# Delta rule inverse on 64 by 64 diagonal blocks in opposite quarters of TensorE, with a later channel mean and six earlier taps

## The reference

```
def gated_delta_rule_chunked(q, k, v, g, beta):
    ...
    L = jnp.where(strict, jnp.einsum('nbhid,nbhjd->nbhij', kb, kc) * decay, 0.0)
    eye = jnp.eye(CHUNK, dtype=jnp.float32)
    rhs = jnp.concatenate([vc * bc[..., None], kb * jnp.exp(gc)[..., None]], axis=-1)
    sol = lax.linalg.triangular_solve(eye + L, rhs, left_side=True, lower=True, unit_diagonal=True)
    ...

def hybrid_mixer(...):
    ...
    c = jax.nn.glu(cfm_in, axis=-1)
    c = causal_dwconv(c, cfm_dw_w) + cfm_dw_b
    c = jax.nn.silu(layernorm(c, cfm_ln_g, cfm_ln_b))
    return jnp.concatenate([o_gdn, c], axis=-1) @ w_out
```

## Time and profile before

| | us |
|---|---|
| median of 3 runs | 2077.14 |
| lowest and highest run | 2076.63, 2080.01 |
| the profiled execution, its own time | 2076.46 |
| its span (first to last instruction) | 2074.7 |
| TensorE busy in the span | 2043.9 |
| the inverse, from the last gdn tile to `within(0)` | 1381.1 to 1439.7 |
| the state loop, to the first channel matmul | 1439.7 to 1477.35 |

### The profile page before, as it was taken

How to read it: one execution, slowest core, us unless ns; L and a number is a source line. 1 busy time by engine, 2 the same in 40 slices (tenths; PEclk the granted TensorE clock), 3 DMA queues, 4 the chain that set the end, 5 groups by cost and what they waited for, 6 DMA issues and landing times.

```text
span 2074.7 us, 27847 instructions
## 1 busy us (share of the span) xinstructions
PE 2043.9 (99%) x10022; PEld 1670.7 (81%) x10022; DVE 926.3 (45%) x1180; ACT 891.8 (43%) x1094; POOL 897.8 (43%) x412
## 2 busy tenths in 40 slices
PE   9999999999999999999999999999999999999998
PEld 5888878787878788888888887788898778888887
DVE  4344434354545444511113247877571267555313
ACT  4566652323232332433332247687653335444321
POOL 3232234342424244444444447769265134444443
PEclk9999999999999999999999999999999999999999
DMA  8121123433343332232332332210244123232331
GB/s 332 60 63 60 61 77 111 142 106 142 106 140 107 137 96 91 85 98 91 101 100 93 111 93 70 71 62 2 80 144 124 39 82 100 93 96 96 101 102 61
DMA packets 56383, 203.78 MB, mean 98 GB/s; under 512 B 6256, under 2 KB 8432, under 8 KB 54896
## 3 DMA queue, kind: packets, MB, share of 16 engines
q1 hardware_dynamic: 56304, 202.70, 29.6%
HBM read 200.57 MB, written 2.10 MB: 98 GB/s over the span
## 4 chain that ended last, share of the span: by engine, by line
PE 78%; issue 8%; DVE 5%; POOL 5%; ACT 3%; DMA 0%; POOLq 0%; DVEq 0%; SPq 0%; ACTq 0%
PE acc L2045 18%; PE acc L2047 18%; PE acc L2046 18%; PE aux L2045 5%; PE aux L2047 4%; PE aux L2046 4%; POOL w_lo L525 3%; POOL cfy L550 2%; PE acc L2346 2%; PE aux L2244 1%; DVE qkvf L1718 1%; PE aux L2242 1%; PE aux L2336 1%; PE aux L2257 1%; PE acc L2231 1%
## 5 line engine op out<-in xcount | busy, mean ns | idle before, releaser
L525 POOL TENSOR_TENSOR w_lo<-raw,w_hi 128x1024 fp32r<-128x1024 f32 x317 | 773.6, 2445 | 1123.8 <-ACT w_hi L584 1123.0
L584 ACT ACTIVATE w_hi<-raw 128x1024 fp32r<-128x1024 f32 x317 | 335.3, 1060 | 538.8 <-PE acc L2047 402.2
L2045 PE MATMUL acc<-x_hi,w_hi 128*128 128x512 f32 (+1 forms) x1336 | 523.9, 392 | 6.0 <-DVE x_lo L1463 2.2
L2047 PE MATMUL acc<-x_hi,w_lo 128*128 128x512 f32 (+1 forms) x1336 | 517.7, 387 | 0.0
L2046 PE MATMUL acc<-x_lo,w_hi 128*128 128x512 f32 (+1 forms) x1336 | 517.1, 387 | 0.0
L2045 PEld LDWEIGHTS acc<-x_hi,w_hi 128*128 128x128 f32 x1336 | 251.3, 188 | 62.4 <-DVE x_lo L1463 4.8
L2047 PEld LDWEIGHTS acc<-x_hi,w_lo 128*128 128x128 f32 x1336 | 251.1, 188 | 52.0
L2046 PEld LDWEIGHTS acc<-x_lo,w_hi 128*128 128x128 f32 x1336 | 251.4, 188 | 49.9 <-issue 0.5
L1491 DVE TENSOR_TENSOR ht<-acc,tn 128x512 f32<-128x512 f32 x21 | 14.5, 691 | 173.9 <-PE acc L2047 171.3
L1220 DVE SCALAR_TENSOR_TENSOR adac<-ada,c_act,adac 128x1024 f32<-128x1024 f32 x28 | 40.5, 1446 | 91.9 <-DMA ada<-in_ada 91.4
L2045 PE MATMUL aux<-x_hi,w_hi 128*128 128x512 f32 x192 | 74.9, 390 | 0.8 <-POOL w_lo L525 0.8
(11 more groups left out here) (520 smaller groups left out, 3621.0 us busy)
## 6 DMA issues: line engine op xcount, KB each, us to landing
raw<-in_weights SPq DMA_DIRECT2D x324, 512.0 KB, 3.6
ada<-in_ada SPq DMA_DIRECT2D x32, 512.0 KB, 3.7
ada<-in_ada_first SPq DMA_DIRECT2D x8, 1024.0 KB, 12.1
resid<-in_x SPq DMA_DIRECT2D x2, 1024.0 KB, 6.3
out<-resid SPq DMA_DIRECT2D x16, 128.0 KB, 1.7
decay<-in_tables SPq DMA_DIRECT2D x4, 256.0 KB, 3.4
memf<-in_mem SPq DMA_DIRECT2D x1, 1024.0 KB, 5.1
angles<-in_tables SPq DMA_DIRECT2D x1, 512.0 KB, 4.0
```

Source lines behind the costliest of these rows:

```text
L525: nc.gpsimd.tensor_tensor(lo_home(u), raw[s][:], hi_home(u).bitcast(F32), ALU.subtract).then_inc(lo_ready, 1)
L584: return nc.scalar.activation(out, in_, func, **kw)
L2045: M(out, a_hi, b_hi, start=first, stop=False)
L2047: return M(out, a_lo, b_hi, start=False, stop=last)
```

## The change

The inverse is taken on two 64 x 64 diagonal blocks per chunk and head. The five lower levels work on each block alone: every product becomes two matmuls with 64 rows, 64 weight columns and 64 data columns, one in the upper left quarter of the array, one in the lower right. `xm`, `zs` and the new `xp` hold the blocks packed, 256 columns instead of 512. The transposes become matmuls with the identity. Up to level 4 `x_new` goes into the packed `xp`; the last copies go back to `xt` in two halves. In the last level only the block below the diagonal is computed, in one quarter, scaled by -1 and copied into `xt`.

The taps are spread anew: ScalarE and POOL take three instead of two in each of the conv tiles k = 6 to 11, ScalarE one instead of 1 or 2 in each step of the inverse, and the rest in the state loop. VectorE does fewer in the inverse and more before `within(1)`. `channel_mean` moves from c = 1 to c = 2, `channel_squares` from c = 2 to c = 3, with the steps of ScalarE and VectorE that belong to them.

```
-TN_TAPS, LATE_TAPS = 8, 42
+MORE_FROM = 6
+TN_TAPS, LATE_TAPS = 8, 48
...
+HB = P // 2
+PACK = GDN_H * HB
...
# halves
+    for l in range(1, LEVELS - 1):
+        halves[HB:P, l * P:l * P + HB] = halves[HB:P, l * P + HB:(l + 1) * P]
...
# POOL
-                    cfm_taps(EARLY_POOL)
+                    cfm_taps(EARLY_POOL + (KVQ + MORE_FROM <= j - AHEAD < GATE))
...
# ScalarE, conv tiles
-                cfm_taps(EARLY_POOL)
+                cfm_taps(EARLY_POOL + (k >= MORE_FROM))
...
-                        own["x_first"].own(f(xm[:, c, :], aux[:, c * T:(c + 1) * T]))
+                        own["x_first"].own(f(xm[:, c, :], aux[:, c * T:c * T + PACK]))
...
+            def take_turned(n):
+
+                c, turned = n % NB, aux[:, (4 + n % 2) * T:(4 + n % 2) * T + PACK]
+                own["x_turned"].next()
+                if n < (LEVELS - 3) * NB:
+                    own["x_new"].own(f(xp[:, c, :], turned))
+                    return
+                for r in QUARTER:
+                    ins = f(xt[c].rearrange("p (h n) -> p h n", h=GDN_H)[r, :, r],
+                            turned[r, :].rearrange("p (h n) -> p h n", h=GDN_H))
+                    (own["x_new"] if r.start else step).own(ins)
...
-                cfm_taps(2 if n % 4 else 1)
+                cfm_taps(1)
                 if n < (LEVELS - 2) * NB:
-                    own["x_turned"].next()
-                    own["x_new"].own(f(xt[n % NB], aux[:, (4 + n % 2) * T:(5 + n % 2) * T]))
-
-
-            cfm_taps(len(taps))
+                    take_turned(n)
+
...
# ScalarE, state loop
             new_values(0)
             w_turned(1)
+            cfm_taps(2)
             take_output(0)
+            cfm_taps(2)
             new_values(1)
             w_turned(2)
+            cfm_taps(2)
             output_root(0)
             take_output(1)
+            cfm_taps(len(taps))
             output_hi(0)
             new_values(2)
             w_turned(3)
+            output_root(1)
+            take_output(2)
+            output_hi(1)
+            new_values(3)
             for k in range(CFM_T):
                 own["cfc_ready"].next()
                 own["cfsq_ready"].own(f(cfin[:, k, 0:T], cfy[:, k, :], ACT.Square))
-            output_root(1)
-            take_output(2)
-            output_hi(1)
+            output_root(2)
+            take_output(3)
...
# VectorE, inverse
+                if n < n_solve - NB:
+                    pattern = halves[:, 1 + n // NB, 0:HB].rearrange("p (a n) -> p a n", a=1).broadcast_to([P, GDN_H, HB])
+                    own["zs_ready"].own(V.tensor_tensor(heads(zs[:, n % 2, :]), heads(product_), pattern, ALU.mult))
+                else:
+                    own["zs_ready"].own(V.tensor_scalar(zs[HB:P, n % 2, :], product_[HB:P, :], -1.0, None, ALU.mult))
...
-                elif n % 2 == 0 and n < 20 or n in (17, 19):
+                elif n % 3 == 1:
                     cfm_taps(1)
...
-                    own["x_upd"].own(V.tensor_tensor(xm[:, c, :], xm[:, c, :], aux[:, (2 + b) * T:(3 + b) * T], ALU.subtract))
+                    own["x_upd"].own(V.tensor_tensor(xm[:, c, :], xm[:, c, :], aux[:, (2 + b) * T:(2 + b) * T + PACK], ALU.subtract))
                 else:
-                    own["x_upd"].own(V.tensor_tensor(xt[c], xt[c], aux[:, (4 + b) * T:(5 + b) * T], ALU.subtract))
+                    own["x_upd"].own(V.tensor_copy(heads(xt[c])[0:HB, :, HB:P], heads(aux[:, (4 + b) * T:(4 + b) * T + PACK])[0:HB]))
...
# VectorE, state loop
             next_state(0)
-            cfm_taps(1)
+            cfm_taps(2)
...
             gated_output(0)
+            next_state(2)
+            output_low(0)
             own["cfsum_done"].next()
             for k in range(CFM_T):
                 own["cfc_ready"].own(V.scalar_tensor_tensor(cfy[:, k, :], bank(At(T0["mix_out"])), -1.0 / (CFM_T * P),
                                                             cfy[:, k, :], ALU.mult, ALU.add))
-            next_state(2)
-            output_low(0)
-            within(3)
+                if k == 0:
+                    within(3)
...
# TensorE
+            def quarters(bk, lhs, rhs):
+
+                for h in range(GDN_H):
+                    for r in QUARTER:
+                        m = M(packed(aux[:, bk * T:bk * T + PACK], h, r), lhs(h, r), rhs(h, r), start=True, stop=True)
+                return m
...
+            def coupling(n):
+
+                c, b = n % NB, n % 2
+                if n < early:
+                    return quarters(b, lambda h, r: block(bt[:, c, :], h, r, r), lambda h, r: packed(xm[:, c, :], h, r))
+                upper, lower_ = QUARTER
+                for h in range(GDN_H):
+                    m = M(packed(aux[:, b * T:b * T + PACK], h, lower_), block(bt[:, c, :], h, upper, lower_),
+                          packed(xm[:, c, :], h, upper), start=True, stop=True)
+                return m
...
-                    each(2 + b, xt[c], zs[:, b, :]).then_inc(S["xz_done"], 1)
+                    inverse = (lambda h, r: block(xt[c], h, r, r)) if n < NB else (lambda h, r: packed(xp[:, c, :], h, r))
+                    quarters(2 + b, inverse, lambda h, r: packed(zs[:, b, :], h, r)).then_inc(S["xz_done"], 1)
...
# turn_back
-                    m = nc.tensor.transpose(aux[:, b * T + h * P:b * T + (h + 1) * P], xm[:, c, h * P:(h + 1) * P], ident)
+                    for r in QUARTER:
+                        m = M(packed(aux[:, b * T:b * T + PACK], h, r), packed(xm[:, c, :], h, r), ident[r, r],
+                              start=True, stop=True)
...
-                each(n % 2, bt[:, n % NB, :], xm[:, n % NB, :]).then_inc(S["zz_done"], 1)
+                coupling(n).then_inc(S["zz_done"], 1)
...
-                if c == 1:
+                if c == 2:
                     channel_mean()
...
-                if c == 2:
+                if c == NB - 1:
                     channel_squares()
```

More of the change, by code:

```diff
@@ L311, in build_program @@
         ngc, egc, bg, egl = [gcols[:, n, :] for n in range(4)]
-        (xm, zs), _ = overlay(x_at, ("xm", (P, NB, T), F32), ("zs", (P, 2, T), F32))
+        (xm, xp, zs), _ = overlay(x_at, ("xm", (P, NB, PACK), F32), ("xp", (P, NB, PACK), F32), ("zs", (P, 2, PACK), F32))
+        QUARTER = [slice(0, HB), slice(HB, P)]
         nwt, vnew = [bt[:, 0, :], bt[:, 1, :]], [bt[:, 2, :], bt[:, 3, :]]
@@ L1009, in _ @@
                 own["cfsq_ready"].own(f(cfin[:, k, 0:T], cfy[:, k, :], ACT.Square))
-            output_root(1)
-            take_output(2)
-            output_hi(1)
+            output_root(2)
+            take_output(3)
             own["stat_ready"].next()
             roots(bank(At(T0["mix_out"] + 1)), 1.0 / (CFM_T * P), bank(At(T0["mix_out"] + 1)), own["rs_ready"])
-            new_values(3)
-            output_root(2)
-            take_output(3)
             for k in range(CFM_T):
@@ L1776, in _ @@
             gate_tile(3)
+            n_solve = (LEVELS - 1) * NB
             def keep_halves(n):
+                product_ = aux[:, (n % 2) * T:(n % 2) * T + PACK]
                 own["zz_done"].next()
-                own["zs_ready"].own(V.tensor_tensor(heads(zs[:, n % 2, :]), heads(aux[:, (n % 2) * T:(n % 2 + 1) * T]),
-                                                    repeat(halves[:, 1 + n // NB, :]), ALU.mult))
-            n_solve = (LEVELS - 1) * NB
+                if n < n_solve - NB:
[3 more added lines that the diff above has]
+                    own["zs_ready"].own(V.tensor_scalar(zs[HB:P, n % 2, :], product_[HB:P, :], -1.0, None, ALU.mult))
             apart.append(True)
@@ L2541, in turn @@
                 for h in range(GDN_H):
-                    m = nc.tensor.transpose(aux[:, c * T + h * P:c * T + (h + 1) * P], xt[c][:, h * P:(h + 1) * P], ident)
+                    for r in QUARTER:
+                        m = M(aux[r, c * T + h * HB:c * T + (h + 1) * HB], xt[c][r, h * P + r.start:h * P + r.stop],
+                              ident[r, r], start=True, stop=True)
                 m.then_inc(S["x_turned"], 1)
@@ L2611, in _, with packed, block @@
             early = n_solve - NB
+            def packed(x, h, r):
+                return x[r, h * HB:(h + 1) * HB]
+            def block(x, h, r, q):
+                return x[r, h * P + q.start:h * P + q.stop]
+            def quarters(bk, lhs, rhs):
[12 more added lines that the diff above has]
+                return m
             def update(n):
@@ L2617, in update @@
                 if n < early:
-                    each(2 + b, xt[c], zs[:, b, :]).then_inc(S["xz_done"], 1)
-                else:
-                    each(4 + b, zs[:, b, :], xt[c]).then_inc(S["xz_done"], 1)
+                    inverse = (lambda h, r: block(xt[c], h, r, r)) if n < NB else (lambda h, r: packed(xp[:, c, :], h, r))
+                    quarters(2 + b, inverse, lambda h, r: packed(zs[:, b, :], h, r)).then_inc(S["xz_done"], 1)
+                else:
+                    upper, lower_ = QUARTER
```

(4 more changed lines are left out.)

## The result

The changed kernel takes 2087.69 us (median of 6 runs, 2084.86 to 2088.81) against 2076.88 us before on the same chip (6 runs, 2076.33 to 2080.01): a ratio of 1.0047, 95% interval 1.0036 to 1.0057. It is 10.8 us slower where 3.4 us less were forecast, and it lies above the range of 2064 to 2083. The profiled execution took 2088.75 us, 12.3 more than the profiled one of before. One run of all, in experiment 4, was slow (2543.67 us, mean granted clock 0.749 against 0.993 or 0.994 in the others there); without it that median is 0.01 us lower.

What follows compares the result with a forecast made beforehand. TensorE was taken to set the pace, with POOL binding too in the inverse's steady part. Terms -14.4 + 1.0 + 1.0 + 8.0 + 1.0 = -3.4 gave 2073.1, forecast 2073.7 us as median; 8-in-10 range 2064 to 2083.

Steps and rivals of the forecast that it cites:

- The clock's price in the state loop: State loop: each of the two TensorE waits can lower the clock for the mean or gated matmuls; cost 1.0 (0 to 3).
- 1.0 us in the inverse: Inverse: the new 3.7 us gap should bring the lower clock once, over some 1.3 steps; cost 1.0 (0 to 2).
- The state loop itself: From `within(0)` to the first channel matmul: 45.7 us against 37.65 today; cost 8.0 (2 to 10).
- Both waits: State loop: TensorE waits 4.7 us for POOL's last tap before the mean, 4.0 for VectorE before the third `output_sums`.
- The inverse: Start, steady part and last level of the inverse together gain 14.4 us, before the clock's cost.
- The pitch: Steady part of the inverse: a step takes 1.70 us instead of 2.45, over 17 steps.
- the end: Last level of the inverse: 4.7 us from the last turning-back instead of 7.16, a gain of 2.5.
- the query decays: Steady part of the inverse: query decays held by POOL add 1.0 us.
- The early taps: Conv tiles 6 to 11: six taps moved ahead hold VectorE's SBUF-only operations while POOL works; cost 1.0 (0 to 3.5).
- A: Inverse: quarter records don't run at 0.028 us (issue limit, taking turns or low clock); kernel takes 2088.6 us; chance 0.17.
- B: After the inverse: waits are small, `output_low(0)` finds POOL free (-2.3), clock holds (-2); 2069.4 us; chance 0.22.
- C: Conv tiles: early taps hold VectorE in each of six tiles, 3.5 instead of 1.0; 2076.2 us; chance 0.11.

Runs made afterwards that it cites:

- experiment 4: Changed kernel with VectorE's `gated_output(1)` ahead of `next_state(2)` and the channel subtractions, `output_low(0)` behind them: 2080.55 us.
- experiment 3: Changed kernel with five unread matmuls before the wait for POOL's last tap and five before the third `output_sums`: 2083.14 us.
- Experiment 9: Kernel before with only the six early taps, made in conv tiles 6 to 11: 2078.65 us, ratio 1.0011.
- experiment 8: Changed kernel with `gated_output(1)` first, query decays in steps 2 and 3, no early taps, three weight splits moved to steps 5, 9, 13: 2072.29 us.
- experiment 2: Old 128-column inverse with the new schedule alone (new places of taps, mean and squares): 2093.77 us, ratio 1.0076.
- experiment 10: New inverse, taps, mean and squares placed as before; query decays in steps 2 and 3, ScalarE's three splits in steps 5, 9, 13: 2079.02 us.
- experiment 1: Changed kernel with the new inverse alone; taps, mean and squares back in their old places: 2077.54 us, ratio 0.9998.

## Why the prediction was wrong

**The clock's price in the state loop is the step that failed.** The prediction gave the lower level 1.0 us in the inverse, which is what it cost there, and 1.0 us in the state loop, as if only the matmuls right behind a wait ran slower. Set TensorE's `within(0)` to 0. Forecast, the changed kernel, and the traced execution of experiment 3, in which the clock didn't fall from 1340 to 1494 us, stand as follows (each measured time is the start of the row less 1433.65 or 1430.83):

| start of | forecast | after | experiment 3 |
|---|---|---|---|
| the mean | 21.0 | 23.3 | 21.6 |
| third `output_sums` | 33.9 | 38.4 | 34.8 |
| the squares | 37.1 | 43.6 | 37.7 |
| first channel matmul | 45.7 | 54.5 | 48.1 |

Up to the squares, the forecast made without the clock is within 0.9 us of the run in which the clock held. The changed kernel lies 6.4 us above that run at the end. So the clock cost 6.4 where 1.0 was allowed. Of these, 1.7 stand there before the mean, from the fall right behind the inverse (1433.50 to 1437.00), which no term had; 4.7 come behind the two waits. Another 1.5 us follow behind the first channel matmul, where the row of 1488.00 shows half speed as well. It costs so much because TensorE sets the pace between the waits: the outputs, gated matmuls and squares behind each wait run late too, not the mean alone. The 6.4 compare one execution with one other. In the medians filling gave 4.6 us, and by their mean granted clocks the other eleven filled runs kept part of the falls; which part is open, since they have no traces.

**The state loop itself** was sized 8.0 and measured 48.1 - 37.65 = 10.4. Both waits and their causes were right (POOL's last tap; VectorE behind `output_low(0)`, which POOL's splits held for 2.45 us). The missing 2.4 are mostly behind the squares: VectorE puts `gated_output(2)` between the first and the other three channel scalings and starts the first low half only after all four, so that TensorE waits 2.56 us there, where 0.6 had been seen.

**The inverse** gained 10.6 where 13.4 (14.4 less 1.0 of clock) were forecast. The start gained 0.2, as said. The pitch was 1.74 for 1.70, 0.7 over 17 steps; the end, from the turning-back at 1428.62 to 1433.65, is 5.03 us and gained 2.1 for 2.5; the two slow steps behind the wait cost 1.0, as allowed. The term that was mis-sized most is the query decays: three steps of 2.65 us cost 2.7 instead of 1.0, a figure that the prediction gave without working, since such an operation takes 1.70 us beside POOL and sits ahead of the subtraction on VectorE. The fourth cost nothing.

**The early taps** cost 2.6 instead of 1.0 up to the last gate eviction, or 2.1 against the other kernels with the new inverse; both lie within the bounds given (0 to 3.5). Experiment 9 shows them alone; of its 2.7 us, 1.8 reach the end there.

The sum of the misses: 5.4 + 1.5 of clock, 2.4 state loop, 2.8 inverse, 1.6 taps, and 1.9 that the profiled execution had from its start, 15.6, where 15.7 lies between -3.4 and +12.3 (rounding). In the medians the miss is 14.0 (2087.69 against 2073.7), since the profiled execution was one of the slower ones.

**The rivals.** A's time, 2088.6, is within 1 us of the one that came, by luck and not by its mechanism: the records ran at 0.028 us, and the clock was 0.95 over 1396 to 1430. B was wrong: the waits were as long as forecast. C's 3.5 was too much, as the sum's 1.0 was too little. The range ended at 2083 because the clock was bounded at 2 us in the inverse and 3 in the state loop; the row that could have shown more was there, since the trace of before has one low stretch behind one gap of 1.91 us, and the forecast named three longer gaps. Of the two rules weighed, the floor of about 25 ns in the Trainium skill, "TensorE: Matmul & The Clock Gate", section "Wait — 56ns, not 53.3ns?", agrees with the 0.028 us measured; its 62 ns for hardware decode off doesn't show here.

## What to carry to other kernels

A wait of the engine that sets the pace can have two prices: its own length, and what a lowered clock does to everything up to the next wait for another engine. Here 4.39 and 4.09 us of waiting came with 4.7 us more behind them, and ten unread matmuls in the waits were worth 4.6 us of the median. One trace isn't enough to price it: of two executions with nearly the same gap one fell and the other didn't, so look at the mean granted clock of every run. When a loop gets shorter on one engine, count the work of the next one first (POOL had 34.9 us of it in 37), and move that work only to places where the traces show the other engines idle. Then look at what stands in the queue ahead of the first thing that the faster loop needs: three splits moved out of its way gave 4.1 us by themselves (from 1.1 to 5.2 us below the kernel before).

## What the runs showed of the hardware

- Opposite quarters of TensorE (64 x 64 each, F32) run side by side: 16 records in 0.45 us, 0.028 us apart and each 0.22 us long, with the weight loads beside them. One quarter alone, in the last level, has a record every 0.058 us (five from 1426.12 in the kernel after take 0.45 us).
- After gaps of 3.38, 4.39 and 4.09 us the granted clock is 0.51 in the rows, for 3.4 to 7 us, and lies low through part of the wait already (1454.00 to 1461.00, with the mean only from 1456.93). After two gaps of 1.71 and 1.74 us it stayed at 1.00 (experiment 8); after one of 1.91 us it had fallen before the edit.
- The length of a gap alone doesn't decide it. Behind 3.38 us (after) the clock fell and behind 3.39 us at the same place (experiment 3) it stayed at 1.00; behind 2.31 us near 1353 it fell in the kernel after and stayed in experiment 2; behind 1.91 us it fell before and behind 1.93 us it stayed in experiment 10.
- The clock also fell in or right behind the last level of the inverse, where only one quarter works: 0.52 in 1433.50 to 1437.00 after, 0.54 in experiment 1, 0.66 in experiment 8. In the changed kernel no gap just ahead was longer than 0.95 us, in the two experiments some were of 1.3 to 1.9. The old inverse with the new schedule (experiment 2) showed 1.00 from 1386 to 1440, but so did experiment 3 with the same quarters as the changed kernel. Whether the quarters, the gaps between them or something else lowers it there stays open.
- An operation of VectorE on SBUF tiles took 2.45 us beside POOL's weight splits (1464.31) and 0.69 when POOL stood (1472.71).
